# Attention inside a streamed-weights trunk: values stationary, probabilities scaled before the transposes

## What is computed

```python
def window_attention(q, k, v, sinks, bias):
    # 16 query heads of 64 features, 4 key/value heads; chunks of 64 positions see themselves and the chunk before
    kb, vb = band(k), band(v)
    logits = jnp.einsum('bnigrd,bnjgd->bngrij', q, kb) * (HEAD_DIM ** -0.5) + bias
    logits = jnp.where(valid, logits, NEG_INF)
    probs = jax.nn.softmax(jnp.concatenate([logits, sink_col], axis=-1), axis=-1)[..., :-1]
    out = jnp.einsum('bngrij,bnjgd->bnigrd', probs, vb)
    return out.reshape(b, s, ATTN_WIDTH)

# in each layer
y_a = window_attention(q, k, v, attn_sinks[i], bias) @ w_attn_out[i]
...
y_c = (sc_b * causal_dwconv(sc_c * sc_h, sc_conv[i])) @ w_sc_out[i]
x = x + (g0 * y_a + g1 * y_b + g2 * y_c) @ w_mix_out[i]
```

## Time and profile before

| | us |
|---|---|
| median of 3 runs | 1199.96 |
| lowest, highest | 1199.86, 1200.32 |
| profiled execution, its own time | 1199.09 |
| profiled execution, span from first to last instruction | 1197.4 |
| TensorE busy in the span | 1138.7 |
| VectorE, ScalarE, GpSimd busy | 795.6, 690.2, 423.7 |

### The profile page before, as it was taken

How to read it: one execution, slowest core, us unless ns; L and a number is a source line. 1 busy time by engine, 2 the same in 40 slices (tenths; PEclk the granted TensorE clock), 3 DMA queues, 4 the chain that set the end, 5 groups by cost and what they waited for, 6 DMA issues and landing times.

```text
span 1197.4 us, 26929 instructions
## 1 busy us (share of the span) xinstructions
PE 1138.7 (95%) x9340; PEld 1123.3 (94%) x9340; DVE 795.6 (66%) x1163; ACT 690.2 (58%) x1101; POOL 423.7 (35%) x405
## 2 busy tenths in 40 slices
PE   5789999999998999999979999999999989999996
PEld 4689999999998999999979999999999989999996
DVE  6377887786756555456678787779676655545556
ACT  5267988765644443443647688877475444434453
POOL 0098777893003000002127786789510300000012
PEclk8989999999999999999999999999999989999998
DMA  5745433455454455445335453435545535545540
GB/s 210 264 142 186 167 107 142 158 194 185 177 180 172 144 193 212 157 175 212 141 115 196 172 186 111 141 125 195 182 178 192 195 120 193 183 174 177 209 142 36
DMA packets 29241, 201.78 MB, mean 169 GB/s; under 512 B 3504, under 2 KB 3696, under 8 KB 5568
## 3 DMA queue, kind: packets, MB, share of 16 engines
q1 hardware_dynamic: 27504, 195.38, 45.7%
q0 software_dynamic: 1088, 4.74, 1.2%
q10 hardware_dynamic: 528, 0.15, 0.1%
HBM read 199.18 MB, written 3.69 MB: 169 GB/s over the span
## 4 chain that ended last, share of the span: by engine, by line
PE 80%; issue 8%; DMA 4%; ACT 3%; DVE 2%; POOL 2%; ACTq 0%; POOLq 0%; DVEq 0%
PE bank L313 24%; PE bank L315 24%; PE bank L314 23%; PE bank L348 2%; PE bank L349 2%; DMA rel_bias_rows<-rel_bias_by_distance 2%; PE bank L351 2%; POOL pacc L1189 2%; DMA bias<-rel_bias_rows 1%; PE bank L416 1%; DMA idt<-in_ident 1%; DVE rstd L830 1%; DVE w_lo L821 1%; ACT cprod L527 1%; ACT cv L706 1%
## 5 line engine op out<-in xcount | busy, mean ns | idle before, releaser
L313 PE MATMUL bank<-h_hi,w_hi 128*128 128x256 f32 x1856 | 531.2, 286 | 15.3 <-ACT gated L598 13.4
L314 PE MATMUL bank<-h_lo,w_hi 128*128 128x256 f32 x1856 | 525.8, 283 | 0.0
L315 PE MATMUL bank<-h_hi,w_lo 128*128 128x256 f32 x1856 | 525.7, 283 | 0.0
L821 DVE TENSOR_TENSOR w_lo<-w_raw,w_hi 128x2048 fp32r<-128x2048 f32 x183 | 432.0, 2363 | 95.2 <-ACT w_hi L527 92.2
L527 ACT ACTIVATE w_hi<-w_raw 128x2048 fp32r<-128x2048 f32 (+1 forms) x185 | 351.1, 1900 | 142.0 <-DMA w_raw<-in_wstream 100.2
L313 PEld LDWEIGHTS bank<-h_hi,w_hi 128*128 128x128 f32 x1856 | 356.6, 192 | 21.2 <-issue 18.7
L314 PEld LDWEIGHTS bank<-h_lo,w_hi 128*128 128x128 f32 x1856 | 356.8, 192 | 0.1
L315 PEld LDWEIGHTS bank<-h_hi,w_lo 128*128 128x128 f32 x1856 | 356.7, 192 | 0.0
L1189 POOL TENSOR_TENSOR pacc<-pacc,cprod 128x256 f32<-128x256 f32 x280 | 309.1, 1104 | 61.8 <-ACT cprod L527 41.9
L313 PE MATMUL bank<-act_hi,w_hi 128*128 128x256 f32 x896 | 253.9, 283 | 0.0
L314 PE MATMUL bank<-act_lo,w_hi 128*128 128x256 f32 x896 | 253.6, 283 | 0.0
(11 more groups left out here) (130 smaller groups left out, 928.1 us busy)
## 6 DMA issues: line engine op xcount, KB each, us to landing
w_raw<-in_wstream SPq DMA_DIRECT2D x184, 1024.0 KB, 4.8
rel_bias_rows<-rel_bias_by_distance POOLq DMA_DIRECT2D x1, 2560.0 KB, 18.9
bias<-rel_bias_rows POOLq DMA_DIRECT2D x1, 1536.0 KB, 13.2
xs<-in_x SPq DMA_DIRECT2D x2, 512.0 KB, 4.7
out_y<-xs SPq DMA_DIRECT2D x4, 256.0 KB, 2.1
zacc<-in_p POOLq DMA_DIRECT2D x2, 256.0 KB, 4.3
prms<-in_prm SPq DMA_DIRECT2D x1, 320.0 KB, 10.1
idt<-in_ident ACTq DMA_DIRECT2D x1, 64.0 KB, 7.9
```

The costliest lines, as they stand in the source:

```text
L313: nc.tensor.matmul(o, wh, hi, start=first, stop=False, skip_group_check=True)
L314: nc.tensor.matmul(o, wh, lo, start=False, stop=False, skip_group_check=True)
L315: return nc.tensor.matmul(o, wl, hi, start=False, stop=last, skip_group_check=True)
L821: nc.vector.tensor_tensor(w_lo[:, n % RING, :], w_raw[:, n % RAW_RING, :], f32(w_hi[:, n % RING, :]), ALU.subtract).then_inc(lo_ready, 1)
```

## The change

The value product is turned round: v_tok is now the stationary operand (64 columns for each head) and probs_t the moving one. The result has features on the partitions (head e on partitions 64e to 64e+63 of bank 6) and positions on the free axis, so the output transposes go, with o_tok and their semaphores. The reciprocal sums would now lie along the wrong axis, so they are multiplied into the probabilities before these are transposed, in place, by four tensor_scalar instructions a tile (`scale_probs`). The probability transposes wait for that (probs_scaled) instead of the exponentials. `round_attn` and `low_attn` read bank 6 and run one step sooner, for tile j-2; as they share the bank with the probability transposes, these wait for attn_lo of the tile before. On VectorE the step's order becomes low_attn(j-2), denominators(j-1), scale_probs(j-1), softmax(j), w_lo and the rest.

```diff
                 def probs_transpose(t):
                     for e in range(2):
-                        pe.wait_ge(exp_done, L * 2 * QT + 2 * t + e + 1)
+                        pe.wait_ge(probs_scaled, L * 2 * QT + 2 * t + e + 1)
                         if e == 0 and t > 0:
-                            pe.wait_ge(o_ready, L * QT + t)
+                            pe.wait_ge(attn_lo, L * QT + t)
...
-                        if e == 1 and t > 1:
-                            pe.wait_ge(attn_lo, L * QT + t - 1)
...
-                    for e in range(2):
-                        v = slice((g + e) * HEAD_DIM, (g + e + 1) * HEAD_DIM)
-                        o = [psum[6][:, (b * 2 + e) * HEAD_DIM:(b * 2 + e + 1) * HEAD_DIM] for b in range(TB)]
-                        nc.tensor.matmul(o[0], probs_t[:, e, 0:P], v_tok[:, 0, v], start=True, stop=True)
-                        nc.tensor.matmul(o[1], probs_t[:, e, P:2 * P], v_tok[:, 0, v], start=True, stop=False)
-                        mm = nc.tensor.matmul(o[1], probs_t[:, e, 2 * P:3 * P], v_tok[:, 1, v], start=False, stop=True)
+                    for b in range(TB):
+                        for e in range(2):
+                            rows, v = slice(e * HEAD_DIM, (e + 1) * HEAD_DIM), slice((g + e) * HEAD_DIM, (g + e + 1) * HEAD_DIM)
+                            mm = nc.tensor.matmul(psum[6][rows, b * P:SEQ], v_tok[:, b, v], probs_t[:, e, b * SEQ:SEQ + b * P],
+                                                  start=b == 0, stop=b == 1, skip_group_check=True)
                     mm.then_inc(pv_done, 1)
-
-                def out_transpose(t):
-                    pe.wait_ge(o_ready, L * QT + t + 1)
-                    if t == QT - 1:
-                        pe.wait_ge(attn_lo, L * QT + t)
-                    for b in range(TB):
-                        mm = nc.tensor.transpose(psum[7][:, b * P:(b + 1) * P], o_tok[:, b, :], idt[:, :])
-                    mm.then_inc(ot_done, 1)
...
                 def round_attn(t):
-                    act.wait_ge(ot_done, L * QT + t + 1)
-                    copy(act_hi[:, t, :], psum[7][:, 0:SEQ]).then_inc(attn_hi, 1)
+                    act.wait_ge(pv_done, L * QT + t + 1)
+                    copy(act_hi[:, t, :], psum[6][:, 0:SEQ]).then_inc(attn_hi, 1)
...
-                    if 0 <= j - 3 < QT:
-                        round_attn(j - 3)
+                    if 0 <= j - 2 < QT:
+                        round_attn(j - 2)
...
-                def normalise(t):
+                def scale_probs(t):
 
                     r = t % 2
                     dve.wait_ge(rec_ready, L * QT + t + 1)
-                    dve.wait_ge(pv_done, L * QT + t + 1)
-                    if t > 0:
-                        dve.wait_ge(ot_done, L * QT + t)
-                    rec = smx[:, r, :, :].rearrange("p b e -> p (b e)").unsqueeze(2).to_broadcast([P, 2 * TB, HEAD_DIM])
-                    nc.vector.tensor_tensor(o_tok[:, :, :].rearrange("p b (e d) -> p (b e) d", e=2),
-                                            psum[6][:, 0:2 * P].rearrange("p (c d) -> p c d", d=HEAD_DIM), rec,
-                                            ALU.mult).then_inc(o_ready, 1)
+                    for e in range(2):
+                        for b in range(TB):
+                            cols = slice(0, P) if b == 0 else slice(P + CHUNK, P + SEQ)
+                            last = nc.vector.tensor_scalar(probs[:, r, e, cols], probs[:, r, e, cols], smx[:, r, b, e:e + 1],
+                                                           None, ALU.mult)
+                        last.then_inc(probs_scaled, 1)
...
                     if 0 <= j - 2 < QT:
-                        normalise(j - 2)
-                    if 0 <= j - 3 < QT:
-                        low_attn(j - 3)
+                        low_attn(j - 2)
+                    if 0 <= j - 1 < QT:
+                        denominators(j - 1)
+                        scale_probs(j - 1)
                     if j < QT:
                         softmax(j)
-                    if 0 <= j - 1 < QT:
-                        denominators(j - 1)
```

More of the change, by code:

```diff
@@ L164, in build @@
         probs_t = sb("probs_t", [P, 2, P + SEQ])
-        o_tok = sb("o_tok", [P, TB, P])
         smx = sb("smx", [P, 2, TB, 2])
@@ L233, in build @@
         pv_done = sem("pv_done")
-        o_ready = sem("o_ready")
-        ot_done = sem("ot_done")
+        probs_scaled = sem("probs_scaled")
         attn_hi = sem("attn_hi")
@@ L445, in _ @@
                         weigh_values(j - 2)
-                    if 0 <= j - 3 < QT:
-                        out_transpose(j - 3)
                     if j < QT:
@@ L943, in softmax @@
                             dve.wait_ge(pt_done, L * 2 * QT + head - 3)
-                        if t >= 2 and e == 0:
-                            dve.wait_ge(o_ready, L * QT + t - 1)
                         dve.nop(nofuse=True)
@@ L966, in denominators @@
                     nc.vector.reciprocal(smx[:, r, :, :], srec[:, r, :, :]).then_inc(rec_ready, 1)
-                def normalise(t):
+                def scale_probs(t):
                     r = t % 2
                     dve.wait_ge(rec_ready, L * QT + t + 1)
-                    dve.wait_ge(pv_done, L * QT + t + 1)
-                    if t > 0:
-                        dve.wait_ge(ot_done, L * QT + t)
-                    rec = smx[:, r, :, :].rearrange("p b e -> p (b e)").unsqueeze(2).to_broadcast([P, 2 * TB, HEAD_DIM])
-                    nc.vector.tensor_tensor(o_tok[:, :, :].rearrange("p b (e d) -> p (b e) d", e=2),
-                                            psum[6][:, 0:2 * P].rearrange("p (c d) -> p c d", d=HEAD_DIM), rec,
-                                            ALU.mult).then_inc(o_ready, 1)
+                    for e in range(2):
[4 more added lines that the diff above has]
+                        last.then_inc(probs_scaled, 1)
                 def low_attn(t):
                     dve.wait_ge(attn_hi, L * QT + t + 1)
-                    low(act_lo[:, t, :], psum[7][:, 0:SEQ], act_hi[:, t, :], attn_lo)
+                    low(act_lo[:, t, :], psum[6][:, 0:SEQ], act_hi[:, t, :], attn_lo)
                 def zstep(t, k):
```

## The result

The changed kernel takes 1216.18 us, median of 4 runs (1215.53 to 1216.99), against 1199.91 (1198.96 to 1200.32) for the kernel before on the same chip: ratio 1.0137 [1.0119, 1.0155]. It is slower, as forecast, by 16.3 us where 11.3 were forecast; 1216.2 lies inside the range of 1202 to 1220, and above the forecast's own range, which ended at 1214.6.

A forecast was written before the change was run, and what follows sets the result against it. TensorE, 95% busy, bounded the kernel; after the change a loop of 7.55 + 1.95 = 9.5 us a step would, adding 5.6 us a layer, 11.2 to the median: 1211.2 us. Own range 1207.8 to 1214.6; wider range 1202 to 1220.

The forecast's parts named there:

- Mechanism: Attention stage: transposes wait for scaled probabilities behind low_attn and act_hi; the loop takes 9.5 us a step, hiding TensorE's gain.
- The rival in which TensorE's gain shows: Attention stage: TensorE sets the pace, 16 x 0.66 = 10.6 us gained, 1189.4; needs link under about 0.65; chance 0.09.
- link: From act_hi's end on ScalarE through VectorE and TensorE to the next probs_t copy: 1.95 us, bounds 1.71 to 2.05.
- TensorE's term: New value product without output transposes: TensorE gains 0.66 us a step, bounds -0.2 to +0.86, hidden in the wait.
- the round: ScalarE's own work in one step of the attention stage: 7.55 us.
- Step 1: Scaling while GpSimd is busy: may cost a layer 0 to 0.9 us, as ScalarE has 0.7 in hand.
- the rival on GpSimd: VectorE's scalings held up beside GpSimd's adds: 15 us, 1226; 0.10 together with a tighter VectorE round.
- Tile 1: Its probs_t copy on ScalarE follows act_hi of tile 0 at 141.57 instead of 139.93: 1.64 us late.
- The sum: Attention stage: a layer is 5.6 us longer, two layers 11.2 us.
- the last value product: End of the attention stage on TensorE: gives between -0.2 and +0.4 us, taken as nothing.
- VectorE's round: VectorE's work a step grows from 6.5 to 7.0 us, cover 2.5; costed at nothing, some 0.5 a layer if used up.
- GpSimd's slowing: Both scalings of head 0 held up in each step, 14 x 1.1 = 15 us; 0.10 with a tighter VectorE round.

The follow-up runs named there:

- e4: Kernel before with only the scaling moved ahead of the transposes; value product and output transposes stay, multiplication into o_tok becomes a plain copy: 1214.65 us, ratio 1.0129.
- e1: Changed kernel with ScalarE rounding the output tile (act_hi) ahead of the 1.8 us copy to w_hi: 1208.86 us, ratio 1.0083.
- e3: Changed kernel with VectorE making denominators and scalings ahead of low_attn: 1207.79 us, ratio 1.0076.
- e5: Changed kernel with both moves: act_hi ahead of w_hi on ScalarE, denominators and scalings ahead of low_attn on VectorE: 1202.44 us, ratio 1.003.
- e6: Changed kernel with act_hi ahead of w_hi and the scalings left out, so attention is not normalised: 1190.82 us, ratio 0.9933.
- e7: e1 with ScalarE's copies of the transposed probabilities put behind the first three products for GpSimd: 1208.9 us, ratio 1.0086.
- e12: e5 with two tensor_tensor scalings for four tensor_scalar, and the short convolution's low half on GpSimd: 1201.05 us, ratio 1.0014.

## Why the prediction was right, and what it mis-sized

**Mechanism.** Right in each step that it named. The transposes wait for the scaled probabilities; VectorE waits for act_hi behind w_hi; TensorE waits the saving away. e4 shows that the loss comes with the scaling alone, e1, e3 and e5 that most of it goes when the queues' orders are changed and all work is kept. The rival in which TensorE's gain shows asked for a link under 0.65 us; it was 2.06.

**TensorE's term.** Forecast 0.66 a step, measured 0.71 (e6). The two heads run side by side: in the trace's records their passes start in pairs 7 ns apart. The Trainium skill (TensorEngine Tiling (Array Packing), Theoretical Speedup) offers up to 2x where one side is 64 or smaller. The trace agrees: 8 passes with a stationary side of 64 columns take 0.63 us of weight loads, where 1.29 in a row was estimated.

**The link and the round.** Forecast 7.55 + 1.95 = 9.5 a step. In layer 1 the round is 7.72 and the link 2.06 in the mean, 9.78 together, so six steps are 1.7 us longer than forecast. The link is 2.14 in three of layer 1's seven steps, where srec takes 0.29 to 0.30 instead of 0.15, each time beside an add of GpSimd (as at 150.97 above, against 141.22), and 2.00 in the other four. Of the 0.05 by which these four exceed 1.95, head 0's scaling has 0.03: it takes 0.52 from its start, not 0.49. The forecast read the slope from L957 to L997 as agreeing with twice tensor_tensor's rate. It does not: 0.73 ns a column against 1.03 is 1.4 times. The scalings themselves, 0.286 for 128 columns and 0.314 for 192, come to 0.45 ns a column. Of the round's 0.17, some 0.07 are waits like the 0.26 at 148.01 (0.5 us in the seven rounds of layer 1, by the view of the waits); the rest was not traced.

**Step 1.** Here the sum left out what the rival on GpSimd had named, up to 0.9 a layer in the first step: it took 0, and the trace shows 0.93. With the scaling at 1.75 and srec at 0.69 the first transposes come at 131.07, the second pair at 131.90; ScalarE's copy of head 1 waits 0.34 and w_hi starts 0.93 later. Tile 1's copy comes 2.62 late in layer 1, forecast 1.64: 1.0 more.

**The clock.** Not in the forecast at all. After two stalls of layer 0 TensorE ran at 1.2 GHz, products 0.215 apart instead of 0.12. Some 11 products each time, 0.095 us each, and 0.47 for the slower transposes at 201.02 (1.14 against 0.67) make 2 x 1.0 + 0.5 = 2.5; layer 0's stage is 2.6 longer than layer 1's. The cost is read from rows at both levels, and the table bears it out: the kernels whose stage stayed at 1.00 have equal layers. That the stalls caused the fall was not tested apart, and both layers show like stalls without it.

**The sum.** Layer 1: 5.6 forecast, plus 1.0 (tile 1), plus 1.7 (six steps), less 0.3 (behind the last copy, where the forecast took the last value product at nothing), 8.0; measured 7.95. Layer 0: 2.6 more for the clock, 10.5. Outside the stages the span is 0.8 shorter. It is the time before layer 0's stage, which starts at 117.90 instead of 118.67; in the traces of all kernels here, whose edits all lie in the stage, this start lies between 115.1 and 118.8. 10.5 + 7.95 - 0.8 = 17.7 is the difference of the two spans; that of the medians is 16.3, the two profiled executions lying 0.8 below and 0.6 above theirs.

So the spans differ by 6.5 more than the forecast's 11.2: 2.0 from step 1, 3.4 from the link and the round, 2.6 from the clock, less 0.6 and 0.8. Without the clock's 2.6 the median would be near 1213.6, an estimate from these rows, and inside the forecast's own range, which ended at 1214.6. That 1202 to 1220 held the result is thus in part luck: its width was given for the rivals, not for the clock.

**VectorE's round.** Forecast at "some 0.5 a layer" if its cover were used up, with 2.5 us of cover a step on the mean. In the change that held: it waits for act_hi in every step. But the mean hid that two steps in three are heavy: the heavy step that ends at 150.63 left VectorE 0.32 us to wait, the light one at 140.88 left 4.91. That fits the shortfall of e1, e3 and e7: the next bound was 0.3 us away in the heavy steps, not 2.5.

**GpSimd's slowing.** Given a tenth as a rival, for each step. It did not decide there, as the scaling came in GpSimd's gap in 14 of 16 tiles. It decided the experiments: each new order brought the scaling back under the adds in some of the steps and lost 0.3 to 1.0 us there.

**Open.** A version that is faster than before would need VectorE's heavy steps shorter, by an estimate about a microsecond: 9.48 in e12, against 8.85 before and 8.14 for TensorE alone. Moving the gate or a tap to another engine was not tried.

## What to carry to other kernels

Before work is taken from the busiest engine, close the loops: follow each new wait round all the in-order queues until it meets itself, and compare the lap with the pace of the busiest engine; here a lap of 9.8 us beat 8.14. A mean slack over unlike steps is not a cover; take it from the fullest step. And when an order is changed to hide a VectorE instruction, look at what GpSimd does in the new place.

## What was not expected of the hardware

How much VectorE's instructions lose beside GpSimd depends on where their operands lie, in SBUF or in PSUM. In e5, GpSimd and VectorE:

```profile
747.91 6.02 POOL L1170 TENSOR_TENSOR pacc<-pacc,cprod 128x256 f32<-128x256 f32 x6 [1.58 <-ACT cprod L512]
```

```profile
748.96 0.95 DVE L810 TENSOR_TENSOR act_lo<-prod,act_hi 128x256 fp32r<-128x256 f32 x1
749.84 0.41 DVE L882 TENSOR_TENSOR z<-bank,gated 128x256 f32<-128x256 f32 x1
```

Both have 256 columns and run beside the same chain of adds. The one with both operands in SBUF takes 0.95 us, the one with an operand in PSUM 0.41. Over all of e5 the first kind (act_lo<-prod) takes 0.42 where GpSimd is idle and 0.75 to 0.96 beside it; act_lo<-bank takes 0.41 in both. The tensor_scalar pair of a head, with everything in SBUF, goes from 0.29 and 0.31 to 0.62 and 0.31 in e5: the first is held, the second follows at once. The Trainium skill (SBUF — State Buffer, Who interferes with whom) says that VectorE and GpSimd share a pair of ports as an exclusive lock; VectorE instructions with two SBUF inputs or in a two-port mode contend for it, others with at most one SBUF input do not. The trace agrees: the two operands of 0.95 lie in SBUF, and a scaling is held for part of an add and not slowed in proportion to its size.
